# A hybrid decoder layer on one Trainium2 core: a ring of ten places for the expert weights, a router tail in column parts, an fp32 gather, and products on zeros at the start

## The reference, cut to what matters

```python
h = jnp.concatenate([meta, x], axis=1)
hn = rms_norm(h, attn_norm_w)
u_conv, q_lat, kv_lat, g_lin = jnp.split(hn @ w_in, SPLITS, axis=-1)
y_conv = conformer_conv(u_conv, ...)          # depthwise conv of 31 taps, layer norm, silu, w_pw2
y_mla = mla(q_lat, kv_lat, ...)               # 8 heads, causal, w_o
g = jax.nn.sigmoid(g_lin + gate_b).reshape(B, L, 2, 1024)
h = h + (g[:, :, 0] * y_conv + g[:, :, 1] * y_mla) @ w_out
h = h + moe(rms_norm(h, ffn_norm_w), ...)
return h[:, 16:]

# moe, per token: the four largest of 32 logits, softmax over these four as gates; per expert e:
gu = xb @ w_gate_up[e] + b_gate_up[e]         # 1024 -> 2048
g, u = gu[:, :1024], gu[:, 1024:]
act = (min(g, 7) * sigmoid(1.702 * min(g, 7))) * (clip(u, -7, 7) + 1)
y = (act @ w_down[e] + b_down[e]) * gate      # 1024 -> 1024, summed into the token's row
```

## Time and profile before

| what | value |
|---|---|
| median of 3 runs | 1149.9 us |
| the profiled execution: its time | 1151.61 us |
| its span, first to last instruction | 1149.7 us |
| TensorE (PE) busy | 1063.8 us, 93% |
| VectorE (DVE) busy | 250.0 us, 22% |
| ScalarE (ACT) busy | 170.3 us, 15% |
| bytes moved by DMA | 431.90 MB, mean 376 GB/s |
| SyncE's DMA queue, share of 16 engines | 90.7% |

### The profile page before, as it was taken

The page is one execution under the profiler, slowest core; times in us unless marked ns, Lnnn a source line. Parts: engine busy times, 40 slices in busy tenths (PEclk is TensorE's granted clock), DMA queues, the critical chain, the costliest instruction groups (busy, mean ns, idle before and its releaser), DMA issues.

```text
span 1149.7 us, 15140 instructions
## 1 busy us (share of the span) xinstructions
PE 1063.8 (93%) x6271; PEld 476.3 (41%) x6271; DVE 250.0 (22%) x656; ACT 170.3 (15%) x341; POOL 6.8 (1%) x17
## 2 busy tenths in 40 slices
PE   7999989799999999999999999999999999999996
PEld 5788876533333333333333333333333333333332
DVE  1588742721111111111111111111111111111101
ACT  3453340411100000000000000000000000000000
POOL 1000000000000000000000000000000000000000
PEclk9999999899999999999999999999999999999998
DMA  9843275599999999999999999999999999999995
GB/s 289 301 126 112 74 291 222 182 428 416 427 429 429 428 429 428 428 428 429 428 428 429 429 429 429 427 429 428 382 422 429 429 429 428 429 429 429 428 428 219
DMA packets 52643, 431.90 MB, mean 376 GB/s; under 512 B 5075, under 2 KB 23838, under 8 KB 28174
## 3 DMA queue, kind: packets, MB, share of 16 engines
q1 hardware_dynamic: 51984, 431.04, 90.7%
q0 software_dynamic: 272, 0.43, 0.2%
q10 hardware_dynamic: 366, 0.15, 0.1%
HBM read 430.55 MB, written 1.05 MB: 375 GB/s over the span
## 4 chain that ended last, share of the span: by engine, by line
PE 56%; DMA 39%; ACT 2%; DVE 1%; issue 1%; SPq 1%; ACTq 0%; DVEq 0%
DMA arena<-in_w_down 29%; PE psum L781 17%; PE psum L804 14%; DMA arena<-in_w_gate_up 10%; PE psum L589 5%; PE psum L504 4%; PE psum L814 3%; PE psum L642 2%; PE psum L680 2%; PE psum L751 2%; PE psum L766 1%; ACT arena L1044 1%; PE psum L792 1%; PE psum L759 1%; PE psum L580 0%
## 5 line engine op out<-in xcount | busy, mean ns | idle before, releaser
L781 PE MATMUL psum<-arena 128*64 128x512 f32 x2048 | 448.7, 594 | 9.5 <-DMA arena<-in_w_gate_up 9.0
L804 PE MATMUL psum<-arena 128*64 128x512 f32 x1024 | 233.1, 604 | 51.3 <-DMA arena<-in_w_down 37.1
L781 PEld LDWEIGHTS psum<-arena 128*64 128x64 f32 x2048 | 144.2, 137 | 311.6 <-issue 292.3
L1345 DVE TENSOR_SCALAR arena<-psum 128x512 f32<-128x512 f32 x32 | 22.1, 691 | 760.7 <-PE psum L781 749.9
L804 PEld LDWEIGHTS psum<-arena 128*64 128x64 f32 x1024 | 71.4, 138 | 190.9 <-issue 137.2
L1032 ACT COPY arena<-psum 128x512 f32<-128x512 f32 x32 | 18.7, 585 | 490.8 <-PE psum L751 490.8
L814 PE MATMUL psum<-arena 64*128 64x512 f32 x256 | 63.7, 615 | 0.7 <-ACT arena L1048 0.7
L751 PEld LDWEIGHTS psum<-arena 128*128 128x128 bf16 x1536 | 48.4, 98 | 29.2 <-issue 29.2
L589 PE MATMUL psum<-arena 128*128 128x256 f32 x256 | 58.8, 381 | 0.3 <-ACT arena L963 0.3
L1048 ACT COPY arena<-psum 128x512 f32<-128x512 f32 x32 | 18.7, 585 | 265.9 <-PE psum L804 265.9
L751 PE MATMUL psum<-arena 128*128 128x64 bf16 x1536 | 52.2, 194 | 4.0 <-DVE arena L1278 4.0
(11 more groups left out here) (218 smaller groups left out, 497.0 us busy)
## 6 DMA issues: line engine op xcount, KB each, us to landing
arena<-in_w_gate_up SPq DMA_DIRECT2D x128, 2048.0 KB, 26.2
arena<-in_w_down SPq DMA_DIRECT2D x63, 2048.0 KB, 21.9
arena<-in_w_in SPq DMA_DIRECT2D x9, 1024.0 KB, 6.1
arena<-in_w_in SPq DMA_DIRECT2D x8, 512.0 KB, 9.0
arena<-in_w_out SPq DMA_DIRECT2D x1, 4096.0 KB, 17.2
arena<-in_w_o_mla SPq DMA_DIRECT2D x1, 2048.0 KB, 10.0
arena<-in_conv_pw_w SPq DMA_DIRECT2D x1, 2048.0 KB, 15.9
arena<-in_w_down SPq DMA_DIRECT2D x4, 512.0 KB, 21.0
```

The costliest lines, as they stand in the source:

```text
L781: last = mm(b[64 * half:64 * half + 64, :], xe[i][:, k, :], gu[i][c][:, j, o + half * 512:o + half * 512 + 512], start=(k == 0 and bias_la ...
L804: last = mm(Y[64 * c:64 * c + 64, :], aT[:, j, 64 * h:64 * h + 64], dn[h][:, j, c * 512:(c + 1) * 512], start=(h == 0 and j == 0), stop=(h ...
L1345: ts(g_s, G, LIMIT, None, ALU.min).then_inc(S.g_ready, 1)
```

## The change

It has five parts.

1. **Ring.** The ten places of 2 MB are one ring (`slot_gu`, `slot_dn`, the same memory seen in two shapes). Piece k of the run of six pieces an expert goes to place k mod 10, and waits only until piece k-10 has been used (one semaphore, `used`). The loops over experts go in rounds of five. What the router tail keeps in SBUF (`h1`, `hT`, `mixT`) moves out of the places, so that the ten first pieces can be loaded before the first expert starts; `w_out` comes in two column halves.
2. **Router tail in column parts.** `project_out` makes five parts (`OUT_PARTS`: 512, 512, 512, 256, 256 columns), and squares, transposes and logits follow part by part. `x` is loaded into `h1` and added by VectorE; the four identity products of `residual` now read `h1` and stand late in the tail. The fp32 norm is never written out: its scale is folded into `ph` and its weight `fnw` into the copy of the gathered rows. Places are counted per token tile, and the first expert's gather is split in two (`gather_first`).
3. **Gather.** `gather` multiplies fp32 rows of `h1` (16 products an expert, read with a step of two elements by `row_order`) by an fp32 `ph`. `rows_out` moves from ScalarE to VectorE, where it stands between the clips and the multiplications of `activations`.
4. **Channel sums.** VectorE adds the four channel tiles before the layer norm's products with ones (`channel_sum`), so that one product is left of four, twice.
5. **Products on zeros.** TensorE does three and then five products of 128x256 on a cleared tile (`busy`) before and after the first small transpose. GpSimd clears the tile.

```diff
+PER, RING10 = GC + DC, 10
+ROUND = 5
+SIDE = [0, 1, 0, 1, 2]
+OUT_PARTS = [(0, 0, 512), (0, 512, 512), (1, 0, 512), (1, 512, 256), (1, 768, 256)]
...
             def load(e, piece, slot):
...
+                to = slot_gu[slot] if piece < GC else slot_dn[slot]
+                sp.dma_start(to, src).then_inc(in_slot[slot], 16)
...
+            load(0, 5, 5)
+            for k in (6, 7):
+                load(1, k - PER, k)
+            for k in (8, 9):
+                sp.wait_ge(S.h1_ready, 3 if k == 8 else 5)
+                load(1, k - PER, k)
+            with sp.Fori(0, (E - 2) // ROUND) as it:
+                for m in range(RING10, RING10 + ROUND * PER):
+                    sp.wait_ge(S.used, ROUND * PER * it + (m - RING10 + 1))
+                    load(ROUND * it + m // PER, m % PER, m % RING10)
...
+            def busy(bank, times, n):
+                for _ in range(times):
+                    mm(psum[:, bank, 0:n], idle[:, 0:P], idle[:, 0:n], start=True, stop=True)
+            pe.wait_ge(S.cols_clear, 3)
+            busy(6, 3, SEQ)
...
+            busy(6, 5, SEQ)
...
+            pe.wait_ge(S.lnsum_ready, 1)
+            filled("lnmu", mm(fill("lnmu")[:, 0:SEQ], ones, lnsum[:, 0, :], start=True, stop=True))
...
-            residual(0)
-            residual(1)
...
+            project_out(OUT_PARTS[0], 0, KD)
+            project_out(OUT_PARTS[1], 0, KD)
+            project_out(OUT_PARTS[2], 0, 2)
+            turn_state(OUT_PARTS[0])
...
             def gather(n, i):
                 pe.wait_ge(S.built, n + 1)
+                pe.wait_ge(S.sT_ready, n)
                 for k in range(KD):
                     for t in range(2):
-                        for part in range(3):
-                            last = mm(X[:, k * SLOTS:(k + 1) * SLOTS], xn3[:, t, part, k * P:(k + 1) * P],
-                                      ph[i][:, t, :], start=(t == 0 and part == 0), stop=(t == 1 and part == 2))
+                        last = mm(X[:, k * SLOTS:(k + 1) * SLOTS], row_order(h1[:, t, :])[:, k // GR, k % GR, :],
+                                  ph[i][:, t, :], start=(t == 0), stop=(t == 1))
                 last.then_inc(S.gathered, 1)
...
+            gate_up(0, SIDE[-1], *pieces_of(0), bias_last=True)
+            b = fill("cnt")[:, 0:E]
+            mm(b, ones, maskt[:, 0, :], start=True, stop=False)
+            filled("cnt", mm(b, ones, maskt[:, 1, :], start=False, stop=True))
+            turn(0, SIDE[-1])
...
             def activations(n, after=None, first=False):
+                dve.wait_ge(S.used, PER * n + GC)
                 ts(g_s, G, LIMIT, None, ALU.min).then_inc(S.g_ready, 1)
                 ts(a_s, U, LIMIT, -LIMIT, ALU.min, ALU.max).then_inc(S.a_step, 1)
...
+                if after is not None:
+                    dve.wait_ge(S.gathered, n + 2)
+                    rows_out(after, 0, KD).then_inc(S.xe_ready, 1)
```

More of the change, by code:

```diff
@@ L458, in _ @@
                                ).then_inc(in_bias, 16)
+            with nc.allow_non_contiguous_dma(reason="the norm's weight in the order of the experts' rows"):
+                pool.dma_start(fnw.rearrange("p (c j) -> p c j", j=GR),
+                               a["ffn_norm_w"][0].rearrange("(c p j) -> p c j", c=GC, j=GR)).then_inc(in_bias, 16)
             pool.wait_ge(S.ymix_ready, 4)
@@ L719, in _ @@
[L719 to L723 removed]
+                    ins = mm(b[:, 0:n], mixT[:, k, t * P:(t + 1) * P], wout[c // 512][:, k, c % 512:c % 512 + n],
+                             start=(k == 0), stop=(k == KD - 1))
+                if last == KD:
+                    filled(("ho",) + part, ins)
@@ new lines, in turn_state, with router @@
+            def turn_state(part):
+                t, c, n = part
+                pe.wait_ge(S.h1_ready, OUT_PARTS.index(part) + 1)
+                b = fill(("ht",) + part)
+                for i in range(n // P):
+                    at = c + i * P
+                    last = nc.tensor.transpose(b[:, i * P:(i + 1) * P], h1[:, t, at:at + P], ident)
+                filled(("ht",) + part, last)
+            small_bank = psum[:, 5, :]
+            LG, RANK = (0, E), 2 * E
+            def router(t, first, last):
+                if first == 0:
+                    pe.wait_ge(S.router_ready, 1)
+                    fill(("lg", t))
+                for k in range(first, last):
+                    ins = mm(small_bank[:, LG[t]:LG[t] + E], hT[:, k, :], rwt[:, k, :], start=(t == 0 and k == 0),
+                             stop=(k == KD - 1), skip_group_check=True)
+                if last == KD:
+                    filled(("lg", t), ins)
@@ L859, in _ @@
                     turn(n, 0)
-                    gate_up(n, 0, 16 * j + 16 * (E // 2 + 1))
+                    slots = list(range(PER))
+                    loads = [16 * ((PER * E - 2 - k) // RING10 + 2) + 16 * j for k in slots]
+                    gate_up(n, 0, slots, loads)
                     turn_act(n)
-                    down(n, (16 * j + 16 * (E + 1), 16 * j + 16 * E))
+                    down(n, slots, loads)
                     scatter(n, 0)
```

599 lines of the change are left out of this document (301 added, 298 removed).

## The result

| | before | changed |
|---|---|---|
| median of the comparison | 1150.05 us | 1179.44 us (1178.3 to 1187.34) |
| ratio | | 1.027, interval 1.0226 to 1.0316 |
| profiled execution: time, span | 1151.61, 1149.7 us | 1178.97, 1177.2 us |
| PE busy | 93% | 97% |

The kernel became slower by 2.7%. The forecast was 1168 with a range of 1152 to 1178. The direction and the bound were right, the size was not, and the time lies just outside the range. The longest of the four executions, 1187.34 us, is the one with the lowest mean granted clock, 0.984 against 0.990 to 0.993 in the others.

The account below looks back on a forecast made before the run. The prediction took TensorE (PE) to become the bound, at 29.3 us an expert: expert 1's start at 255.4, plus 30 x 29.3, plus 33.6 for the last expert, gives 1168 us, range 1152 to 1178.

Parts of the forecast that it names:

- What bounds the kernel: Expert stage before: transfers' period 29.38 us, PE's 27.04, so PE has a reserve of 2.34 us an expert.
- I take 0.113 us, near the router's: Pace of the fp32 gather's 32 pieces: 0.113 us each, 3.5 us to the last start, bounds 3.3 and 3.7.
- What follows the gather in the period: Gather to down: VectorE's path 7.35 us, 2.3 more than before; PE's own 7.0; new period 29.3.
- The head: Before the experts: zeros, channel sums and router tail move the first expert from 229.55 to about 218.8 us.
- The first expert: Expert 0: later down biases add 1.8 us, gather and copy 2.3; expert 1's gate-up starts at 255.4.
- The last expert: End of the kernel, no gather: gate-up, down and the rest to the span's end take 33.6 us.
- The transfers' path: Weight stream: without the dip and resuming about 10 us earlier, would end the kernel at 1137, hidden behind PE.
- The first rival: Expert stage: transfers stay the bound if PE's period is under 28.3 us, gather at most 2.4; 1137 us; chance 0.11.
- No change: Whole kernel: head gains and longer period cancel, needing a period of 28.7 us; 1150 us; chance 0.09.
- Weight loads that do not run beside products: Gather: 0.16 us a piece, 5.1 us in all, period 31.0, end at 1219 us; chance 0.03.

Follow-up runs that it names:

- Experiment 3: Kernel before the change with only its gather made 16 fp32 products, weights read with a step of one; 1184.97 us, ratio 1.0294.
- experiment 1: Changed kernel with the gather of experts 1 to 31 made 48 bf16 products on constants again; 1150.91 us, ratio 1.001.
- experiment 5: Changed kernel with VectorE's row copy behind its multiplications and TensorE's `turn` behind down; 1183.2 us, ratio 1.0315.
- experiment 4: Changed kernel without the eight products on zeros; 1182.77 us.
- Experiment 6: Kernel with exchanged operands: changed kernel, gather's places as weights and state streamed, gather of expert 1 earlier, `turn` behind down; 1138.88 us, ratio 0.9926.
- e7_again: Second measurement of the unaltered kernel with exchanged operands, against the kernel before; 1141.1 us, ratio 0.9931.

## Why the prediction was wrong in size and right in kind

**What bounds the kernel: right, the reserve too large.** PE holds 95% of the chain. But the reserve of 2.34 us an expert compares the periods alone and leaves out that PE starts late. PE's own path in the kernel before is 262.14 + 30 x 27.04 + 33.6 = 1106.9, 42.8 us ahead of its end, so 1.4 us an expert were free. Experiment 3 shows the difference: its period, 29.22, is still below the transfers' 29.38, and it lost 34 us (a start 9.8 us later and 30 x 2.18 more, less the 42.8, make 32). The sum itself compared whole paths, so this slip did not enter it. Experiments 1 and 3 show the cause from both sides: without the fp32 gather the loss is gone, and with nothing but the fp32 gather it is all there.

**"I take 0.113 us, near the router's": too low.** This is the first mis-sized term. The pieces start 0.118 us apart, the upper bound, which the row nearest in kind had given: `turn_act`, with a step. The router's 0.107 is a mean of 16 pieces of which the first had its weights loaded ahead, at 205.63; its loads start 0.111 apart, and not 0.117 as the text divides them. To the last start the gather takes 3.70 us, where 3.5 was taken and 3.7 was the bound; the 0.21 from there to the scatter was counted only on VectorE's path (as 0.3). The period is 29.43 (29.44 on average to the last expert) instead of 29.3: 29 x 0.145 = 4.2 us.

**"What follows the gather in the period": the sum right, the reason not.** From gather to down 7.35 was forecast and 7.45 measured. The text had VectorE's chain as the longer path and PE's own at 7.0. In fact PE's own path is 7.45, since its largest piece was sized at 3.5 instead of 3.91, and experiment 5 took VectorE's row copy off its path without any gain. "PE's own path is about as long" was written and then not used: with two paths that close, an error in the shared piece decides which counts.

**The head: the sum right.** 218.8 forecast, 218.20 measured; the tail from the first product with `w_out` is 41.8 us (218.20 - 176.37), 42.2 forecast. The first 16 pieces did fall from 6.04 to 3.69, as forecast, but in experiment 4 they did so without the products on zeros too, so that this term came out right for a reason that was not needed.

**"The first expert": the second mis-sized term.** 255.4 was forecast for gate-up of expert 1, and 258.42 and 257.01 were measured; gate-up itself took 15.58 and 16.22 instead of 13.88. The prediction took 3.63 us for the down biases and copied what followed from a trace in which the clock had also fallen for part of this stretch (down 8.61). It had no term for more of the same, and how long the clock stays down differs from one execution to the next. Expert 2 started at 289.62, against 255.4 + 29.3 = 284.7: 4.9 us. Three rows hold 4.4 of them: the down biases 1.24, down 1.45, gate-up 1.70 us longer.

**The last expert: right** (33.6 forecast, 1177.2 - 1143.52 = 33.7 measured).

Together 4.9 + 4.2 + 0.1 = 9.2, and 1168 + 9.2 = 1177.2, the span. The remaining 2.2 us to the median are the third term: the prediction set the median equal to the span, as it was by chance before, though a profiled execution takes 1.8 to 1.9 us more than its span in both kernels. Without any one of the three the median would have come within the range.

**The transfers' path: right, and hidden as said.** 1137 was forecast; the kernel with exchanged operands, whose period is below the transfers', has a span of 1137.1. That it fits to 0.1 is luck: the last wait for gate-up weights came 11.5 us sooner, not 13.1, another 1.7 is the clock in the last down products, and other executions of the same kernel have spans of 1134.0 to 1142.9. The first rival named the condition, a gather of at most 2.4 us and a period under 28.3. Experiment 6 met it with 2.39 and 27.81 and got the forecast time of that rival.

**The other rivals: excluded.** No change would have needed a period of 28.7, and it is 29.43. Weight loads that do not run beside products would have needed a gather of 5.1 us, and it is 3.91.

## What to carry to other kernels

Before an edit, compare the two whole paths and not only the two periods. Here the periods, 27.04 us of PE against 29.38 of the transfers, promise 2.34 us an expert for nothing. Because PE starts late, 1.4 were free, and past that each tenth of a microsecond is paid once an expert. A mean over a short row hides its first and last step; the distance between starts is the safer figure. Counting products says little about fp32: here 16 fp32 products with large weights and few columns cost 2.6 times what 48 bf16 ones did, and the same work with the small matrix as the weights and the large one streamed costs 1.72 us plus 0.67 for turning the result. A better prefetch ring shows nothing while another engine is late, so it should be measured beside a version in which that engine is fast.

## What the runs showed that was not expected

- **Weights with a step.** Fp32 weights of 128x128 read with a step of two elements are loaded 0.118 us apart, adjacent ones 0.112, both with 64 columns. The estimate of 107 ns in the prediction, from the columns/1.2 ns of the Trainium skill's page "TensorE: Matmul & The Clock Gate", section "LDWEIGHTS (loading the stationary operand)", is lower than either.
- **Instructions loaded.** With 1.03 MB of instructions instead of 0.26 to 0.28 the kernel of experiment 1 took 1150.9 us, where a short loop with less PE work took 1143.2. By volume the 0.75 MB would be under 2 us at 428 GB/s. What the traces show is that the 16 landings of a piece of weights draw 11.9 us apart in it, against 2.9, and that a piece counts only with its last landing. That the instruction loads are what holds some of them back is likely and not isolated.
- **The granted clock in one stretch.** In the profiled executions of the kernels with the new router tail the clock fell between 235 and 265 us, in stretches of several microseconds, but for e7_again, in which it did not. Over the executions of one kernel the span differs by up to 9 us with it (1134.0 to 1142.9). What decides it stays open: neither 3.9 us of gather moved into the waits nor products in two of the waits kept it up.
